# An input projection rewritten as seven half-size block products, with half of its outputs turned afterwards

## Chip, cores and metric

One core of a Trainium2 chip runs the kernel. The metric is the device time of one execution in microseconds (us), the median of several runs. TensorE (PE) does matrix products, and its weight loads are listed apart as PEld; VectorE is DVE, ScalarE is ACT, GpSimd is POOL, and SyncE (SP) issues most of the DMAs.

## Reference

The layer works on 2048 tokens of 1024 features, in float32:

```
mod = silu(c) @ w_ada + b_ada;  shift, scale, gate = split(mod, 3)
h = rms_norm(x, norm_g) * (1 + scale) + shift
u = h @ w_in                                   # 2048 x 1024 times 1024 x 8192
a_q, a_f, a_i, a_g, b_q, b_k, b_v, b_g = split(u)
o_a = rms_norm(hgrn2(silu(a_q), a_f, a_i)) * silu(a_g)
o_b = rms_norm(stick_breaking_attention(b_q, b_k, b_v)) * silu(b_g)
out = rms_norm(x + gate * (concat(o_a, o_b) @ w_out), final_g)
```

The change concerns `h @ w_in`, its outputs' activation and storing, and the making of `h`.

## The kernel before

The kernel runs five stages one after the other: `condition` (makes h), `project` (u), `hgrn`, `stick`, `output`. They hand data on through DRAM.

**Precision.** A float32 product is made of three reduced-precision ones. A number is rounded to a high part (ACT or POOL) and the rest is its difference to that (DVE or POOL); a product is hi\*hi + hi\*lo + lo\*hi.

**condition.** SP loads w_ada (12 pieces of 1 MB) and x (4 groups of 512 tokens). PE makes the modulation (L155). For each group ACT sums squares (L193), DVE scales x (L247), PE transposes it (L169), ACT makes the high part h_hi (L202), DVE makes the full h again (hx, L283) and POOL subtracts to h_lo (L295). h_hi and h_lo for all 2048 tokens stay in SBUF.

**project.** It goes through 32 chunks of 256 columns of w_in, in the order of the list PROJ: four kinds for which the output is feature by token (gq, gf, sq, sk), then four for which it is token by feature (gi, gg, sv, sg), four chunks each. A chunk has eight PSUM tiles of 128x512. For the first 16 chunks w is the stationary operand and 512 tokens move (L361, 24 matmuls a tile). For the last 16, h is stationary and 256 columns of w move (L370, 48 matmuls a tile). SP loads a chunk of 1 MB into the single buffer w_raw (L452), at the tile after POOL has finished splitting the chunk before; POOL splits it (L340, L342) into w_hi and w_lo, which have two buffers each. ACT applies the sigmoid or copies (L399 to L406), DVE finishes the output (L423 to L441), SP stores it (L477). DVE and ACT each take the tile that PE has just finished.

Eight PSUM banks hold eight tiles, so PE waits only for the bank of the tile eight before:

```
def tile(c, j, par, feature):
    pe.wait_ge(u_taken, 8 * c + j + 1)
...
if j == 1 and not (last and par == 1):
    sp.wait_ge(w_split, i * 4 + (2 * par + 2))
    load_w(i * 2 + (par + 1))
sp.wait_ge(u_taken, n + 9)
```

Some rows below are of the stage `output`, for operations of the same kinds: L1217 transposes, L1221 products of 128x512, L1277 rounding on ACT, L1358 the rest on DVE. L726 is a DVE multiplication in `hgrn`.

Of the kernel before, what the change touches and what calls it, by code (L numbers as in the profile page):

```python
# [26 lines left out]
P = 128  # L27
# [14 lines left out]
KO = 2 * D // P  # L42
NLEV = 8
# [19 lines left out]
def condition(nc, io, keep, h_hi, h_lo, w_raw, w_first, sv_rows):  # L63

    with ExitStack() as stack:
# [5 lines left out]
        slots = [n % 3 if n < n_mod + 1 else n % 2 for n in range(n_ada)]  # L71

        def slot(n):
            return ada[:, slots[n]] if slots[n] < 2 else w_raw[:, :, :]
# [5 lines left out]
        ada = m.sb("ada", [P, 2, KD, AC])  # L80
        xg = m.sb("xg", [P, 2, 4, D])
# [10 lines left out]
        hx = m.sb("hx", [P, 2, 512])  # L92
# [5 lines left out]
        x_in = [m.sem(f"x_in{i}") for i in range(2)]  # L98
# [13 lines left out]
        hx_ready = m.sem("hx_ready")  # L112
        lo_ready = m.sem("lo_ready")
        dve_step = m.sem("dve_step")

        with nc.Block() as block:
            @block.sync
            def _(sp):
# [5 lines left out]
                def load_x(g):  # L124
                    if g >= 2:
                        sp.wait_ge(xt_ready, KD * (g - 1))
                    src = io["x"][g * 512:(g + 1) * 512, :].rearrange("(b p) n -> p b n", p=P)
                    sp.dma_start(xg[:, g % 2], src).then_inc(x_in[g % 2], 16)
# [9 lines left out]
                for n in range(6, n_mod + 2):  # L138
                    load_ada(n)
                load_x(2)  # L140
                load_ada(n_mod + 2)
                load_ada(n_mod + 3)
                load_x(3)

                sp.wait_ge(mod_ready, [n for n in range(n_ada) if slots[n] == 2][-1] + 1)
                sp.dma_start(w_raw[:, :, :], io["w_in"][0]).then_inc(w_first, 16)

            @block.tensor
            def _(pe):
# [12 lines left out]
                for g in range(TG):  # L162
                    pe.wait_ge(xn_ready, 4 * (g + 1))
                    for k in range(KD):
                        n = g * KD + k
                        if n >= 4:
                            pe.wait_ge(hx_ready, n - 3)
                        for b in range(4):
                            mm = nc.tensor.transpose(xt_ps[n % 4][:, b * P:(b + 1) * P],  # L169
                                                     xg[:, g % 2, b, k * P:(k + 1) * P], keep["ident"][:, :])  # L170
                        mm.then_inc(xt_ready, 1)
                    modulation(n_mod + g)

            @block.scalar
            def _(act):
# [6 lines left out]
                act.dma_start(keep["g_hgrn"][:, :], io["g_hgrn"].partition_broadcast(P)).then_inc(wide_in, 16)  # L182
                act.dma_start(keep["g_stick"][:, :], io["g_stick"].partition_broadcast(P)).then_inc(wide_in, 16)
                act.dma_start(sv_rows[0:1, :], io["zero"]).then_inc(wide_in, 16)

                def squares(g):
                    act.wait_ge(x_in[g % 2], 16 * (g // 2 + 1))
                    if g >= 1:
                        act.wait_ge(var_ready, g)
                    for b in range(4):  # L190
                        if g or b:
                            act.wait_ge(sq_ready, 4 * g + b)
                        nc.scalar.activation(junk[:, :], xg[:, g % 2, b, :], ACT.Square,  # L193
# [4 lines left out]
                def high(g):  # L198
                    for k in range(KD):
                        n = g * KD + k  # L200
                        act.wait_ge(xt_ready, n + 1)
                        nc.scalar.activation(h_hi[:, k, g * 512:(g + 1) * 512], xt_ps[n % 4][:, :], ACT.Identity,  # L202
# [11 lines left out]
            def _(dve):  # L214
# [20 lines left out]
                def norm(g):  # L235
# [10 lines left out]
                    for b in range(4):  # L246
                        nc.vector.tensor_scalar(xg[:, g % 2, b, :], xg[:, g % 2, b, :], stat[:, 3, b:b + 1], None,  # L247
                                                ALU.mult).then_inc(xn_ready, 1)
# [27 lines left out]
                dve.wait_ge(wide_in, 64)  # L276
                for g in range(TG):
                    for k in range(KD):
                        n = g * KD + k
                        dve.wait_ge(hi_ready, n + 1)  # L280
                        if n >= 2:
                            dve.wait_ge(lo_ready, n - 1)
                        nc.vector.tensor_scalar(hx[:, n % 2, :], xt_ps[n % 4][:, :], mul[:, k:k + 1], shift[:, k:k + 1],  # L283
                                                ALU.mult, ALU.add).then_inc(hx_ready, 1)
                    take_mod(n_mod + g)
                    if 1 <= g < TG - 1:
                        norm(g + 1)

            @block.gpsimd
            def _(pool):  # L290
                for n in range(TG * KD):
                    g, k = n // KD, n % KD
                    pool.wait_ge(hx_ready, n + 1)
                    hi = h_hi[:, k, g * 512:(g + 1) * 512].bitcast(F32)
                    nc.gpsimd.tensor_tensor(h_lo[:, k, g * 512:(g + 1) * 512], hx[:, n % 2, :], hi,  # L295
                                            ALU.subtract).then_inc(lo_ready, 1)


# [5 lines left out]
def project(nc, io, keep, h_hi, h_lo, w_raw, w_first, scr):  # L304

    with ExitStack() as stack:
        m = Mem(nc, stack)
        w_hi = m.sb("w_hi", [P, 2, KD, WC], F32R)
        w_lo = m.sb("w_lo", [P, 2, KD, WC], F32R)
        st = m.sb("st", [P, 2, 512])  # L310
        st2 = m.sb("st2", [P, 2, 512])
        st_hi = m.sb("st_hi", [P, 2, 512], F32R)
        st_lo = m.sb("st_lo", [P, 2, 512], F32R)
        sg = m.sb("sg", [P, 2, 512])
        sg2 = m.sb("sg2", [P, 2, 512])
        u_ps = [m.ps(f"u_ps{i}", [P, 512]) for i in range(8)]

        w_in_sem = m.sem("w_loaded")
        w_high = m.sem("w_high")
        w_split = m.sem("w_split")  # L320
        u_ready = m.sem("u_ready")
        u_act = m.sem("u_act")
        u_taken = m.sem("u_taken")
        g_step = m.sem("g_step")
        staged = m.sem("staged")
        stored = [m.sem(f"stored{i}") for i in range(2)]
        passed = m.sem("w_passed")
        n_pair = NCH // 2

        def tiles():  # L330
            return [(par, j) for par in range(2) for j in range(8)]

        with nc.Block() as block:
            @block.gpsimd
            def _(pool):
                def chunk(c, par):
                    pool.wait_ge(w_in_sem, 16 * c)
                    pool.wait_ge(u_ready, 8 * c + 8)
                    nc.gpsimd.sem_inc(passed, 1)
                    nc.gpsimd.tensor_copy(w_hi[:, par], w_raw[:, :, :]).then_inc(w_split, 1)  # L340
                    pool.wait_ge(w_split, 2 * c + 1)
                    nc.gpsimd.tensor_tensor(w_lo[:, par], w_raw[:, :, :], w_hi[:, par].bitcast(F32),  # L342
                                            ALU.subtract).then_inc(w_split, 1)

                chunk(1, 1)
                with nc.gpsimd.Fori(1, n_pair) as i:
                    for par in range(2):
                        chunk(i * 2 + par, par)

            @block.tensor  # L350
            def _(pe):
                nc.tensor.sem_inc(u_ready, 16)

                def tile(c, j, par, feature):
                    pe.wait_ge(u_taken, 8 * c + j + 1)
                    if feature:
                        cg, tp = j // 4, j % 4
                        n = 0
                        for wt, ht in ((w_hi, h_hi), (w_hi, h_lo), (w_lo, h_hi)):
                            for k in range(KD):  # L360
                                mm = nc.tensor.matmul(u_ps[j][:, :], wt[:, par, k, cg * P:(cg + 1) * P],  # L361
                                                      ht[:, k, tp * 512:(tp + 1) * 512], start=(n == 0), stop=(n == 3 * KD - 1))
                                n += 1
                    else:
                        for b in range(2):
                            tb = 2 * j + b
                            n = 0
                            for wt, ht in ((w_hi, h_hi), (w_hi, h_lo), (w_lo, h_hi)):
                                for k in range(KD):
                                    mm = nc.tensor.matmul(u_ps[j][:, b * WC:(b + 1) * WC], ht[:, k, tb * P:(tb + 1) * P],  # L370
                                                          wt[:, par, k, :], start=(n == 0), stop=(n == 3 * KD - 1))
                                    n += 1
                    mm.then_inc(u_ready, 1)

                for half, feature in ((0, True), (1, False)):
                    with nc.tensor.Fori(half * n_pair // 2, (half + 1) * n_pair // 2) as i:
                        for par in range(2):
                            c = i * 2 + par
                            pe.wait_ge(w_split, 2 * c + 2)
                            for j in range(8):  # L380
                                tile(c, j, par, feature)

            @block.scalar
            def _(act):

                act.wait_ge(w_first, 16)
                for k in range(KD):
                    nc.scalar.activation(w_hi[:, 0, k, :], w_raw[:, k, :], ACT.Copy).then_inc(w_high, 1)
                for t, (name, feature, _) in enumerate(PROJ):
                    with nc.scalar.Fori(t * CH_T // 2, (t + 1) * CH_T // 2) as i:  # L390
                        for par, j in tiles():
# [1072 lines left out]
```

## Time and profile before

| | us |
|---|---|
| median of 3 runs | 3245.58 (3242.29 to 3245.82) |
| the profiled execution | 3247.25 |
| its span | 3245.5 |
| PE busy | 3064.1 (94%) |
| PEld busy | 2722.1 (84%) |
| DVE busy | 1500.2 (46%) |
| ACT busy | 970.9 (30%) |
| POOL busy | 492.1 (15%) |
| mean granted TensorE clock | 0.977 |

The span runs from the first to the last instruction of one execution; busy time is the time in which an engine had an instruction running, so parts of matmuls that overlap are counted once. A granted clock of 1.00 is the 2.4 GHz level, and a value between 0.5 and 1 is a mixture of that and 1.2 GHz over the stretch.

### The profile page before, as it was taken

The page shows a single profiled execution, that of the slowest core. Times are in us where ns is not written, and L with a number is a line of the kernel's source. Part 1 is how long each engine was busy: PE and PEld are TensorE (multiplying, and loading weights), DVE is VectorE, ACT ScalarE, POOL GpSimd, SP SyncE. Part 2 cuts the span into 40 slices and gives each one's busy share as a digit, 9 for nine tenths or more (in the row PEclk, how much of TensorE's full clock was granted, in tenths as well). Part 3 has the DMA queues.
Part 4 walks back from the last instruction along what each step waited for, and adds up shares of the span by engine and source line. Part 5 has one row for each costly group of instructions (what it writes and reads, how often), then busy time and mean ns, then how long its engine had stood idle before and what let it go on. Part 6 is the DMA issues. An engine that isn't in the chain of part 4 may idle for free. (4 is left out here: it accounts for less than half of the span.)

```text
span 3245.5 us, 56894 instructions
## 1 busy us (share of the span) xinstructions
PE 3064.1 (94%) x22432; PEld 2722.1 (84%) x22432; DVE 1500.2 (46%) x1651; ACT 970.9 (30%) x1749; POOL 492.1 (15%) x218
## 2 busy tenths in 40 slices
PE   7899999999999999999788886999999999889998
PEld 5688888888999999999688875887878888778887
DVE  4211221111112221122787885888778887663433
ACT  4211211111111111111011114777767777631111
POOL 3211111111111011100554451000000000000000
PEclk9999999999999999999899997999999999989999
DMA  7113444443222122221544309244533351052221
GB/s 281 50 67 97 122 123 122 120 120 111 73 73 69 60 72 71 68 67 52 190 157 149 113 21 215 65 102 98 131 89 80 95 131 40 24 188 107 84 97 39
DMA packets 217944, 327.14 MB, mean 101 GB/s; under 512 B 11680, under 2 KB 159520, under 8 KB 204960
## 3 DMA queue, kind: packets, MB, share of 16 engines
q1 hardware_dynamic: 217296, 324.08, 33.5%
q8 instruction: 114, 1.87, 0.2%
q10 hardware_dynamic: 464, 0.63, 0.1%
q14 instruction: 70, 0.57, 0.1%
HBM read 207.22 MB, written 117.44 MB: 100 GB/s over the span
## 5 line engine op out<-in xcount | busy, mean ns | idle before, releaser
L1096 DVE TENSOR_TENSOR_SCAN run<-akeep 128x768 f32<-128x768 f32 (+7 forms) x256 | 426.5, 1708 | 134.4 <-ACT akeep L1066 133.7
L1055 ACT ACTIVATE wt<-t_ps 128x512 f32<-128x512 f32 (+3 forms) x640 | 313.6, 534 | 144.6 <-PE t_ps L985 144.4
L985 PE MATMUL t_ps<-ident,run 128*128 128x128 f32 x2176 | 311.5, 278 | 7.0 <-DVE run L1096 6.3
L1066 ACT ACTIVATE akeep<-z_ps 128x1024 f32<-128x1024 f32 (+7 forms) x384 | 289.9, 779 | 75.6 <-PE z_ps L974 68.8
L370 PE MATMUL u_ps<-w_hi,h_lo 128*128 128x256 f32 x2048 | 287.5, 283 | 0.0
L370 PE MATMUL u_ps<-w_lo,h_hi 128*128 128x256 f32 x2048 | 287.5, 283 | 0.0
L370 PE MATMUL u_ps<-w_hi,h_hi 128*128 128x256 f32 x2048 | 287.5, 283 | 0.0
L1005 PE MATMUL o_ps<-wt,ad 128*64 128x128 f32 x4352 | 280.0, 277 | 5.5 <-issue 5.5
L985 PEld LDWEIGHTS t_ps<-ident,run 128*128 128x128 f32 x2176 | 245.1, 141 | 46.7 <-issue 28.3
L969 PE MATMUL z_ps<-ak,aq 128*128 128x512 f32 (+3 forms) x640 | 251.1, 392 | 33.9 <-DMA aq<-s_qlo 33.9
L643 PE MATMUL hps<-hq,hk 128*128 128x128 f32 x1792 | 219.5, 286 | 51.2 <-DVE hq L726 13.5
L1005 PEld LDWEIGHTS o_ps<-wt,ad 128*64 128x64 f32 x4352 | 233.8, 137 | 37.7 <-issue 37.7
L370 PEld LDWEIGHTS u_ps<-w_hi,h_hi 128*128 128x128 f32 x2048 | 264.3, 192 | 0.1
L370 PEld LDWEIGHTS u_ps<-w_hi,h_lo 128*128 128x128 f32 x2048 | 264.2, 192 | 0.0
L370 PEld LDWEIGHTS u_ps<-w_lo,h_hi 128*128 128x128 f32 x2048 | 264.2, 192 | 0.0
L643 PEld LDWEIGHTS hps<-hq,hk 128*128 128x128 f32 x1792 | 214.7, 201 | 55.8 <-issue 53.4
L361 PE MATMUL u_ps<-h_hi,w_hi 128*128 128x512 f32 x1024 | 254.7, 391 | 6.0 <-DVE w_lo L413 6.0
L361 PE MATMUL u_ps<-h_lo,w_hi 128*128 128x512 f32 x1024 | 254.0, 390 | 0.0
L361 PE MATMUL u_ps<-h_hi,w_lo 128*128 128x512 f32 x1024 | 252.9, 389 | 0.0
L974 PE MATMUL z_ps<-ak,aq 128*128 128x512 f32 (+3 forms) x640 | 252.2, 399 | 0.0
L1096 DVE TENSOR_TENSOR_SCAN run<-akeep,run 128x1024 f32<-128x1024 f32 (+1 forms) x128 | 228.4, 1825 | 45.8 <-ACT akeep L1066 45.8
L340 POOL CAST w_hi<-w_raw 128x2048 fp32r<-128x2048 f32 x31 | 58.8, 1895 | 1164.6 <-DMA w_raw<-in_w_in 1164.6
(140 smaller groups left out, 3824.5 us busy)
## 6 DMA issues: line engine op xcount, KB each, us to landing
w_raw<-in_w_in SPq DMA_DIRECT2D x32, 1024.0 KB, 5.5
aq<-s_qhi SPq DMA_DIRECT2D x64, 256.0 KB, 6.3
aq<-s_qlo SPq DMA_DIRECT2D x64, 256.0 KB, 6.8
o<-s_o SPq DMA_DIRECT2D x16, 1024.0 KB, 6.9
ada<-in_w_ada SPq DMA_DIRECT2D x9, 1024.0 KB, 8.5
xg<-in_x SPq DMA_DIRECT2D x4, 2048.0 KB, 11.0
s_gq<-st SPq DMA_DIRECT2D x32, 256.0 KB
s_gf<-st SPq DMA_DIRECT2D x32, 256.0 KB
```

The lines of the kernel that those rows point to most:

```text
L340: nc.gpsimd.tensor_copy(w_hi[:, par], w_raw[:, :, :]).then_inc(w_split, 1)
L361: mm = nc.tensor.matmul(u_ps[j][:, :], wt[:, par, k, cg * P:(cg + 1) * P], ht[:, k, tp * 512:(tp + 1) * 512], start=(n == 0), stop=(n == 3 ...
L370: mm = nc.tensor.matmul(u_ps[j][:, b * WC:(b + 1) * WC], ht[:, k, tb * P:(tb + 1) * P], wt[:, par, k, :], start=(n == 0), stop=(n == 3 * K ...
L643: mm = nc.tensor.matmul(out, k[:, e, toks], q[:, 2 * u + e, toks], start=True, stop=True)
L969: nc.tensor.matmul(zz, q_hi, kk, start=True, stop=False)
L974: mm = nc.tensor.matmul(zz, q_lo, kk, start=False, stop=True)
L985: mm = nc.tensor.transpose(t_ps[a % 2][:, j * P:(j + 1) * P], src[:, key + j * P:key + (j + 1) * P], keep["ident"][:, :])
L1005: mm = nc.tensor.matmul(o_ps[e * SD:(e + 1) * SD, cols], delta[:, b, key // P + j, e * SD:(e + 1) * SD], wt[:, a % 8, j * P:(j + 1) * P], ...
L1055: nc.scalar.activation(wt[:, a % 8, 0:wd], t_ps[a % 2][:, 0:wd], ACT.Identity, scale=-1.0, bias=1.0).then_inc(wt_ready, 1)
L1066: nc.scalar.activation(keepf[:, e, n % 2, 0:width], z_ps[e][:, 0:width], ACT.Sigmoid, scale=-SCALE).then_inc(keep_ready, 1)
L1096: nc.vector.tensor_tensor_scan(run[:, e, qb % 2, at0:at0 + width][:, ::-1], keepf[:, e, n % 2, 0:width][:, ::-1], keepf[:, e, n % 2, 0:width],
```

## The change

`w_in` is cut into blocks of 512 rows by 128 columns, four to a chunk (2 by 2), and h into blocks of 512 features by 512 tokens, four to a pass of 1024 tokens. A 2 by 2 block product is computed with seven products of blocks instead of eight, by sums and differences of the blocks on the way in and of the results on the way out. Each of the seven is again hi\*hi + hi\*lo + lo\*hi: 12 matmuls of 128x512, so a unit ("tile n" below) has 84 matmuls. There are 64 tiles: two passes over the 1024 tokens, 32 chunks each; w_in is loaded in each pass. All outputs are feature by token; for gi, gg, sv and sg PE transposes them in the middle of the next tile's products (`turn`), ACT copies the result out (`turned`), SP stores it.

- In `condition`, h is stored whole (no h_hi, h_lo). Token groups are taken in the order 2, 3, 0, 1; the first two go through four buffers hx to DRAM and are loaded again for the second pass. The x tiles have three buffers; L283 and L295 are gone.
- For each tile, SP loads four blocks of w (two DMAs of 512 KB), POOL makes four combinations (four operations of 128x512, each but one waiting for one before), ACT rounds the seven factors in three operations (`w_rounded`, 1024, 1536 and 1024 columns), DVE makes their rests (`w_rest`, the same three sizes).
- For each pass ACT rounds the seven h factors (2048 columns each), DVE makes three sums and six rests of that size, POOL one rest and one difference.
- For each tile DVE does five sums of 128x512 (PSUM and SBUF into SBUF) besides finishing the four outputs (`shape`).
- The loops are written out, without Fori.

```
+def combine_w(nc, pool, w_raw, t_done, n):
+    w = w_raw[:, n % 2]
+    nc.gpsimd.tensor_tensor(w[:, 3], w[:, 2], w[:, 0], ALU.subtract).then_inc(t_done, 1)
+    pool.wait_ge(t_done, 4 * n + 1)
+    nc.gpsimd.tensor_tensor(w[:, 1], w[:, 6], w[:, 3], ALU.subtract).then_inc(t_done, 1)
+    nc.gpsimd.tensor_tensor(w[:, 2], w[:, 6], w[:, 2], ALU.subtract).then_inc(t_done, 1)
+    pool.wait_ge(t_done, 4 * n + 3)
+    nc.gpsimd.tensor_tensor(w[:, 4], w[:, 5], w[:, 1], ALU.subtract).then_inc(t_done, 1)
...
+            def _(pool):                      # project
+                def build(p):
+                    pool.wait_ge(h_high, 7 * p + 1)
+                    nc.gpsimd.tensor_tensor(hc_lo[:, 0], x[:, 1], hc_hi[:, 0].bitcast(F32), ALU.subtract).then_inc(h_first, 1)
+                    pool.wait_ge(h_sum, 3 * p + 1)
+                    nc.gpsimd.tensor_tensor(x[:, 2], x[:, 1], x[:, 2], ALU.subtract).then_inc(h_third, 1)
+                build(0)
+                for n in range(1, NT):
+                    pool.wait_ge(w_in_sem[n % 2], 32 * ((n + 1) // 2))
+                    combine_w(nc, pool, w_raw, t_done, n)
+                    if n == NCH:
+                        build(1)
...
+            def _(pe):
+                def product(n, j):
+                    pe.wait_ge(w_split, 3 * n + PIECE_OF[j] + 1)
...
+                    if j == 4:
+                        pe.wait_ge(sum_ready, 5 * n + 2)
...
+                for n in range(NT):
+                    for j in range(NP7):
+                        product(n, j)
+                        if n >= 1 and not feature(n - 1) and 1 <= j <= 4:
+                            turn(n - 1, j - 1)
...
+            def _(act):
+                def w_rounded(n):
+                    act.wait_ge(t_done, 4 * (n + 1))
...
+                    for a, b in PIECES:
+                        nc.scalar.activation(w_hi[:, n % 2, a:b], w_raw[:, n % 2, a:b], ACT.Copy).then_inc(w_high, 1)
...
+                for n in range(NT):
+                    if n == NCH:
+                        for j in range(1, NP7):
+                            h_rounded(1, j)
+                    act.wait_ge(u_ready, 7 * n + 1)
+                    wait_free(act, n, 1)
+                    nc.scalar.activation(s_buf[1][:, n % 2, :], b1[n % 2][:, :], ACT.Copy).then_inc(one_ready, 1)
+                    if n >= 1 and not feature(n - 1):
+                        for q in range(4):
+                            turned(n - 1, q)
+                    if n + 1 < NT:
+                        w_rounded(n + 1)
+                    if n == NCH - 1:
+                        h_rounded(1, 0)
+                    for q in range(4):
+                        shape(n, q)
...
+            def _(dve):
+                h_sums(0)
+                for piece in range(3):
+                    w_rest(0, piece)
+                h_rests(0)
+                for n in range(NT):
+                    if n == NCH:
+                        h_sums(1)
+                        h_rests(1)
+                    summed(n, 0)
+                    summed(n, 1)
+                    summed(n, 2)
+                    summed(n, 3)
+                    shape(n, 0)
+                    if n + 1 < NT:
+                        w_rest(n + 1, 0)
+                        w_rest(n + 1, 1)
+                    shape(n, 1)
+                    shape(n, 2)
+                    if n + 1 < NT:
+                        w_rest(n + 1, 2)
+                    summed(n, 4)
+                    shape(n, 3)
...
+            def _(sp):
+                def load_w(n):
+                    if n >= 2:
+                        sp.wait_ge(u_ready, 7 * (n - 1))
...
+                for n in range(NT):
+                    if n + 1 < NT:
+                        load_w(n + 1)
+                    back = n - 1 if n >= 1 and not feature(n - 1) else None
+                    for i in range(4):
+                        if n == NCH - 1:
+                            load_h(i)
+                        if back is not None:
+                            store(back, i)
+                    if feature(n):
+                        for q in range(4):
+                            store(n, q)
```

`sum_ready` counts the sums of `summed`, `w_split` the operations of `w_rest`, `fa_ready` and `fd_ready` the outputs that ACT and DVE have done. `store(n, q)` waits until output q of tile n is finished; gf, sq and sk store two arrays for each output, gq one. For them the gate buffer sg has two places, each free again when its store has landed. A `summed(n, 2)` feeds output 0, `summed(n, 4)` output 3.

## Rows read from the trace of the kernel before

**Rows 1.** The page: busy time of TensorE, and its granted clock in 40 slices.

```profile
PE 3064.1 (94%) x22432; PEld 2722.1 (84%) x22432; DVE 1500.2 (46%) x1651; ACT 970.9 (30%) x1749; POOL 492.1 (15%) x218
...
PEclk9999999999999999999899997999999999989999
```

**Rows 2.** Busy time by stretch: length, PE, PEld, DVE, ACT, POOL, clock, DMA share, GB/s.

```profile
80.00:100.00 20.00, 11.52 (x56) 9.87 (x54) 12.66 (x22) 9.78 (x16) 13.04 (x12) 0.83 0.00 0
...
120.00:796.00 676.00, 676.00 (x2984) 559.95 (x2983) 110.67 (x156) 91.19 (x157) 104.09 (x32) 1.00 0.36 109
800.00:1530.00 730.00, 730.00 (x6071) 729.38 (x6070) 139.84 (x187) 75.79 (x127) 97.71 (x30) 1.00 0.20 68
```

**Rows 3.** Timeline of PE, seam and end of the projection: start, length, engine, line.

```profile
796.32 1.98 PE L361 MATMUL u_ps<-h_hi,w_lo 128*128 128x512 f32 x8
...
803.57 1.12 PE L370 MATMUL u_ps<-w_hi,h_hi 128*128 128x256 f32 x8
...
1539.88 1.12 PE L370 MATMUL u_ps<-w_lo,h_hi 128*128 128x256 f32 x8
```

**Rows 4.** The chain that ended last, in `output`: start, length, what.

```profile
3001.97 1.75 PE ot_ps L1217 x16
3003.72 21.78 PE y_ps L1221 x96
3025.50 1.75 PE ot_ps L1217 x16
```

**Rows 5.** Timeline from the third token group to the start of the projection.

```profile
72.32 5.57 ACT L202 ACTIVATE h_hi<-xt_ps,shift,mul 128x512 fp32r<-128x512 f32 x7 [4.99 <-PE xt_ps L169]
...
89.14 5.69 ACT L202 ACTIVATE h_hi<-xt_ps,shift,mul 128x512 fp32r<-128x512 f32 x7 [4.99 <-PE xt_ps L169]
...
90.84 9.87 POOL L295 TENSOR_TENSOR h_lo<-hx,h_hi 128x512 fp32r<-128x512 f32 x8 [6.96 <-DVE hx L283]
...
101.04 2.56 ACT L388 ACTIVATE w_hi<-w_raw 128x256 fp32r<-128x256 f32 x8 [5.24 <-PEq L116]
...
104.39 3.77 PE L361 MATMUL u_ps<-h_hi,w_hi 128*128 128x512 f32 x8 [5.95 <-DVE w_lo L413]
...
110.87 1.99 PE L361 MATMUL u_ps<-h_hi,w_lo 128*128 128x512 f32 x8
```

**Rows 6.** Single lines: duration in ns, shortest/median/longest, first and last start.

```profile
L342 POOL TENSOR_TENSOR w_lo<-w_raw,w_hi x31: 4598/4613/4629, 124.3 to 1465.0; 128x2048 fp32r<-128x2048 f32 x31
...
L429 DVE TENSOR_SCALAR st<-sg,lb x32: 485/487/4859, 288.4 to 456.7; 128x512 f32<-128x512 f32 x32
...
L726 DVE TENSOR_TENSOR hq<-hq,hf x8: 2264/2274/2284, 1568.6 to 1857.6; 128x2048 f32<-128x2048 f32 x8
...
L1277 ACT ACTIVATE wo_hi<-wo_raw x16: 1055/1062/1067, 2852.5 to 2880.0; 128x1024 fp32r<-128x1024 f32 x16
...
L1358 DVE TENSOR_TENSOR wo_lo<-wo_raw,wo_hi x16: 1218/1225/1227, 2853.6 to 2881.1; 128x1024 fp32r<-128x1024 f32 x16
```

**Rows 7.** Groups of instructions by line: busy us, mean ns, idle before and releaser.

```profile
L295 POOL TENSOR_TENSOR h_lo<-hx,h_hi 128x512 fp32r<-128x512 f32 x32 | 39.5, 1278 | 60.8 <-DVE hx L283 60.8
...
L439 DVE TENSOR_TENSOR st<-u_ps,sg 128x512 f32<-128x512 f32 x64 | 44.3, 691 | 266.1 <-ACT sg L406 266.1
...
L404 ACT ACTIVATE sg<-u_ps 128x512 f32<-128x512 f32 x64 | 38.3, 598 | 330.4 <-PE u_ps L370 330.4
```

**Rows 8.** DMA issues: line, count, KB each, median us from issue to landing.

```profile
w_raw<-in_w_in SPq DMA_DIRECT2D x32, 1024.0 KB, 5.5
...
ada<-in_w_ada SPq DMA_DIRECT2D x9, 1024.0 KB, 8.5
...
hk<-s_gk SPq DMA_DIRECT2D x8, 1024.0 KB, 4.8
...
out<-wo_raw SPq DMA_DIRECT2D x16, 512.0 KB, 2.7
```

**Rows 9.** Timeline of SP's queue in the projection.

```profile
203.57 0.36 SPq L452 DMA_DIRECT2D w_raw<-in_w_in  x1
```

More of the change, by code:

```diff
@@ L42 @@
 KO = 2 * D // P
+KH = KD // 2
+NP7 = 7
+HALF = SEQ // 2
 NLEV = 8
@@ L275, in _ @@
                 dve.wait_ge(col_ready, 1)
-                dve.wait_ge(wide_in, 64)
+                dve.wait_ge(wide_in, 80)
                 for g in range(TG):
[L278 to L285, printed above, removed]
@@ L319, in project @@
         w_high = m.sem("w_high")
         w_split = m.sem("w_split")
-        u_ready = m.sem("u_ready")
[L322 to L331, printed above, removed]
+        h_raw = [m.sem(f"h_raw{i}") for i in range(4)]
@@ new lines, in project @@
+        h_high = m.sem("h_high")
+        h_first = m.sem("h_first")
+        h_third = m.sem("h_third")
+        h_sum = m.sem("h_sum")
+        h_split = m.sem("h_split")
+        u_ready = m.sem("u_ready")
+        one_ready = m.sem("one_ready")
+        sum_ready = m.sem("sum_ready")
+        fa_ready = m.sem("fa_ready")
+        fd_ready = m.sem("fd_ready")
+        t_ready = m.sem("pt_ready")
+        t_taken = m.sem("pt_taken")
+        u_stored = [[m.sem(f"u_stored{q}{j}") for j in range(2)] for q in range(4)]
@@ new lines, in project, with kind, feature @@
+        sg_stored = [m.sem(f"sg_stored{j}") for j in range(2)]
+        stt_stored = [m.sem(f"stt_stored{j}") for j in range(2)]
+        NT = 2 * NCH
+        PIECES = [(0, 2), (2, 5), (5, 7)]
+        PIECE_OF = [0, 0, 1, 1, 1, 2, 2]
+        SUMS = {0: 3, 1: 4, 3: 5}
+        QUAD = {0: (1, 1), 1: (1, 0), 2: (0, 0), 3: (0, 1)}
+        def kind(n):
+            return PROJ[n % NCH // CH_T]
+        def feature(n):
+            return kind(n)[1]
+        fa_at, fd_at, t_at, u_st, sg_st, sg_last, sg_free = {}, {}, {}, {}, {}, {}, {}
@@ new lines, in project @@
+        fa_n = fd_n = t_n = 0
+        for n in range(NT):
+            name = kind(n)[0]
+            for q in range(4):
+                if name not in ("gi", "sv") or q == 2:
+                    fa_n += 1
+                    fa_at[n, q] = fa_n
+                if name not in ("gi", "sv"):
+                    fd_n += 1
+                    fd_at[n, q] = fd_n
+                    sg_free[n, q] = sg_last.get(q % 2)
+                    sg_last[q % 2] = (n, q)
+                if feature(n):
+                    u_st[n, q] = sum((x, q) in u_st for x in range(n % 2, n, 2)) + 1
+                    if name != "gq":
+                        sg_st[n, q] = sum(y[1] % 2 == q % 2 for y in sg_st) + 1
+                else:
+                    t_n += 1
+                    t_at[n, q] = t_n
@@ new lines, in _ @@
+                for n in range(NT):
+                    if n + 1 < NT:
[6 more added lines that the diff above has]
+                            store(back, i)
+                    if feature(n):
+                        for q in range(4):
+                            store(n, q)
@@ L489, in hgrn @@
+                for q in range(4):
+                    store(NT - 1, q)
+                for q in range(4):
+                    for e in range(2):
+                        sp.wait_ge(u_stored[q][e], 16 * max(v for (n, r), v in u_st.items() if r == q and n % 2 == e))
+                for e in range(2):
+                    sp.wait_ge(sg_stored[e], 16 * max(v for (n, q), v in sg_st.items() if q % 2 == e))
+                    sp.wait_ge(stt_stored[e], 16 * (len(t_at) // 2))
 def hgrn(nc, io, keep, scr, o_scr):
```

468 lines of the change are left out of this document (288 added, 180 removed).

## The prediction

> **What bounds the kernel now.** I read the page first: TensorE is busy 94% of the span at nearly the full granted clock, VectorE, the next engine, 46% [rows 1]. Then the busy time by stretch: from 120 to 796 us (outputs feature by token) and from 800 to 1530 us (token by feature) PE is busy all the time at clock 1.00, the 2.4 GHz level, while DVE and ACT are busy under a fifth of it [rows 2]. So the projection costs what its matmuls cost, and fewer matmuls pay in full as long as PE stays fed. Then PE's timeline for the pace: 32 matmuls of 512 columns from 796.32 to 803.57 us are 226.6 ns each; the 6144 of 256 columns from 803.57 to 1539.88 + 8 x 0.12 = 1540.84 us are 120.0 ns each [rows 3], with the weight loads busy throughout [rows 2]. Two of 256 columns cost 240 ns where one of 512 costs 226.6: the second half is the dearer one.
>
> **Matmuls.** At 226.6 ns the first half's 3072 matmuls are 696.1 us; counted back from 803.57 the projection effectively starts at 107.5 (really at 104.4; the first 16 matmuls, after 6 us of PE idle, take 6.5 us, 0.4 us each, the 1.2 GHz level [rows 5]). It thus takes 1540.8 - 107.5 = 1433.3 us. After: 64 tiles x 84 = 5376 matmuls x 226.6 ns = 1218.2 us. Transposes: 32 turned tiles x 16; the output stage runs 16 of them in 1.75 us between products of 21.78 us, and the two add up to the period of 23.53 [rows 4], so 56.0 us. A split into four groups of four might cost a little more; I add nothing. A plain tile is 19.05 us, a turned one 20.8. **Difference: 1274.2 - 1433.3 = -159.1 us**, if PE never waits.
>
> **condition.** A token group takes 16.8 us (72.32 to 89.14 [rows 5]); its chain is ACT's rounding, ACT's squares, DVE's scaling, the transposes, and it stays. Gone is POOL's tail: the last L295 ends at 100.7, some 5 us after ACT's last rounding, and the project block starts at 101. The first group, now paced by ACT and stores (2.7 us landing of a larger one [rows 8], four buffers: about 0.9 us each) instead of by POOL at 1.23, gains no more than the 1 to 2 us that the second loses to its own stores. The block starts near 95. The combination of w for tile 0 is covered by the groups.
>
> **The first tile.** Prices: DVE 2.27 us for 2048 columns, 1.22 for 1024 [rows 6], 1.7 for 1536 between them; POOL 4.61 for 2048 [rows 6], 1.28 for 512 [rows 7]; ACT 1.06 for 1024 [rows 6], about 1.95 for 2048, 0.60 for 512 [rows 7]. In order on DVE before the sums that product 4 needs: two sums (4.5), three rests of w (4.0), four rests of h (9.0), a difference and two rests (6.8), two sums of 512 (1.4, [rows 7]): 26 us, and at least 3 more for POOL's difference in the chain: 29. That is the lower bound. The upper one comes from POOL and DVE in each other's way: a DVE operation of 487 ns once took 4.859 us, as long as POOL's 4.61 [rows 6]. POOL has two operations of 4.6 us and four of 1.28 here, so up to 10 more. By the Trainium skill, "SBUF — State Buffer", "Who interferes with whom", a DVE instruction with two SBUF inputs or in a two-port mode and a POOL instruction reading SBUF exclude each other; that would give the upper bound, and the rule without it the lower. I take +7 (nearer the row of 4.859): product 4 at 95 + 36 = 131, tile 0 ends 8.2 later at 139.2, effective start 120.1 instead of 107.5: **+12.6 us** (6 to 16).
>
> **The seam of the passes.** After tile 31 the same DVE work stands ahead of product 4 of tile 32, less the rests of w but behind 2 us of tile 31's last output: product 4 near 26.5 us after the seam instead of 11 to 12, so +14, and with POOL up to +24. **+20 us.**
>
> **The loop that I think decides.** Follow the order on each queue in a feature tile n. SP issues load_w(n+1) only after store(n-1,3), which waits for DVE's last output of tile n-1; call that moment 0. SP: hop 0.15, a store, the load (an issue is 0.36 [rows 9], some 0.45 with the gap): 0.6. The 1 MB lands in 5.5 [rows 8], 0.2 more for the second DMA: 6.3. POOL: four operations of 1.28 [rows 7] = 5.1, to 11.4. ACT rounds (0.94 + 1.38 + 0.94, the pace behind durations of 1.06 for 1024) to 14.7, and only then does output 0 (0.60): 15.4. DVE: output 0 (0.69), rest of w, first piece (1.22): **17.3, when PE may begin tile n+1**. Second piece 1.7, outputs 1 and 2 1.4, third piece 1.15, last sum 0.7: 22.3. ACT 0.6, DVE 0.7: **23.6, the last output of tile n, which releases load_w(n+2)**. This is a ring of one tile that doesn't contain PE: it turns in 23.6 us where PE needs 19.05. For gq. For gf the last output has two stores ahead of the load (+0.4, and 256 KB more in the queue, +0.6), ACT two sigmoids on outputs 0 and 3 (+1.2), DVE two operations instead of one (0.49 + 0.54, +0.3 x 4), and output 2 waits for output 0's store (+0.4): 27.4. For sq and sk: second store +1.0, waits for the stores of sg +0.7: 25.3. PE then idles in each feature tile. The first and the last of a pass's 16 feature tiles nearly escape; 3 x 4.5 + 4 x 8.3 + 7 x 6.2 = 90, plus 1, and two passes give **+182 us**. The mean ring of the 28 tiles is 25.5 us.
>
> The unknowns: the load lands in 4.8 (hk, an idle queue) to 8.5 us (ada, a full one) [rows 8], 28 tiles x -0.7 to +2.8 = -20 to +78; I take 5.7, as the projection's own row has it. POOL's 512 is a quarter of L342 (1.15) to 1.28: -14 us. A store's landing is not shown for 256 KB; 0 to 2 us per gf, sq, sk tile: -15 to +30. POOL works at 6.3 to 11.4, when DVE only reads PSUM with one SBUF operand, so I charge no collisions.
>
> **Turned tiles.** Here load_w goes at the tile's start (its stores come a tile later) and is covered. ACT however must copy out all four turned outputs before it rounds w: the fourth is turned at 5 x 2.72 + 1.75 = 15.35; ACT 0.6 + 3.3 + 0.6, DVE 0.7 + 1.2: 21.8 against 20.8. For gg and sg, 16 tiles: **+17 us** (0 to 30). gi and sv have no output 0 in that place: nothing.
>
> **Clock.** After 6 us of PE idle the first 16 matmuls ran at 1.2 GHz, and lost 16 x 0.18 = 2.8 us [rows 5]. In the loop a slow start is covered: 19.05 + 2.8 = 21.9 is still under 23.6. A whole tile at that level would be 84 x 0.4 = 34 us and is not.
>
> The last four outputs and their longer tail: +1. hgrn, stick and output are as they were.
>
> **Sum:** -159.1 + 12.6 + 20 + 182 + 17 + 1 = +73.5 us. Span 3245.5 becomes 3319; the profiled execution's own time is 3247.25, 1.7 above the median shown, so against the median 3319.5.
>
> **Rivals.**
> 1. *The loads are hidden as meant.* Were the ring under 19 us (a landing near 1 us, or another order on SP), only ramps and gates would remain: -159.1 + 12.6 + 20 + 17 + 1 = -108.5, or 3137. For it: w has two buffers now, POOL is 15% busy [rows 1]. Against it: 4.8 us is the shortest landing of 1 MB in the rows [rows 8], and ACT and DVE alone hold 12 us of the ring. By the Trainium skill, "Trainium Kernel Development and Optimization", "Best Practices", double buffering overlaps DMA with compute; here the second buffer waits behind the stores on SP. Chance 0.07.
> 2. *The other side: the ring binds, but is shorter, and the kernel gains.* The sum is +73.5; 28 tiles must each be 2.6 us shorter to undo that, a mean ring under 22.9 us instead of 25.5. Its place is the link from the load to POOL's last combination (11.4 us of it). With the landing at 4.8 and POOL at 4.6, and no waits for the stores of sg, the ring is 1.9 us shorter on average, -53 us; both ramps at their lower bounds give 13 more and the gate tiles 17: 73.5 - 83 = -9.5, or 3236. Every one of them has to come out at its favourable end. Chance 0.10.
> 3. *The clock decides.* If with 4 to 8 us of idle per tile the lower level holds through the feature tiles, as in the stretch of clock 0.83 where PE was busy 58% [rows 2], PE needs 34 us: +8.5 x 28 = +240, or 3555. With a mixture at 0.83 it needs 23 and hides. Chance 0.03.
> 4. *The load lands late* (8.5, stores ahead of it in the queue): +78, about 3398. Chance 0.07.
>
> **Numbers.** Forecast (slower, the ring) 0.73, its own range 3265 to 3375. The range reaches down into rival 2 and a little into rival 4: 3235 to 3380 leaves out rivals 1 and 3, half of the others and the forecast's tails, some 0.2. What a measurement of this kernel can tell from no change is about 0.2%, 6.5 us. Faster: rival 1 and most of 2, 0.14; same 0.03; slower 0.83.
>
> **What would show it.** Tile starts on PE 23 to 27 us apart in feature tiles, about 22 or less in turned ones; PE waiting at product 0 for DVE's rest of w; ACT's w_rounded waiting for POOL; POOL waiting for the load; SP's load_w about 0.6 us behind the last output. Matmuls at 226 ns, 84 in 19 us. Wrong would be: feature tiles at 19 to 20 us (rival 1), the clock under 0.8 there (rival 3), landings over 7 us (rival 4), or a wait on sums at products 1 to 6 in mid-pass, which I have nowhere.

## Result and the profile after

The changed kernel takes 3365.45 us (3362.61 to 3368.54, 4 runs) against 3245.7 us: ratio 1.0371, 95% interval 1.0353 to 1.0389. It is slower by 120 us; the forecast was 74 slower, and 3365 lies inside its range. The profiled execution has a span of 3366.2 us.

The page of the changed kernel, for [rows 1]:

```profile
PE 2992.5 (89%) x19104; PEld 2509.7 (75%) x19104; DVE 1887.7 (56%) x2013; ACT 1279.8 (38%) x2090; POOL 615.1 (18%) x384
...
PEclk8798899999898898999899997999999999989999
```

PE has less to do, but is busy 89% instead of 94%, and in the slices of the projection the clock row has 8 and 9 where it had only 9. Busy time by stretch, changed kernel, columns as in [rows 2]: the first stretch holds feature tiles, the second turned ones, the third feature tiles of the second pass.

```profile
180.00:500.00 320.00, 266.79 (x1057) 214.69 (x1057) 126.91 (x167) 83.12 (x114) 64.35 (x51) 0.90 0.41 118
560.00:880.00 320.00, 313.11 (x1481) 255.50 (x1479) 129.41 (x144) 113.99 (x156) 78.79 (x60) 1.00 0.33 106
1000.00:1300.00 300.00, 244.76 (x976) 196.66 (x975) 120.64 (x157) 81.59 (x112) 56.30 (x44) 0.90 0.43 120
```

PE is idle for 17 to 18% of the feature stretches and for 2% of the turned one. DVE, the next engine, is busy 40% there and the DMA engines 41 to 43%, so none of them is full either. That points to a chain through several engines. Who ended PE's idle time between 80 and 1680 us (waits: line, waited for, us in total, times, longest):

```profile
PE b_ps L470 <- DVE w_lo L581: 164.9, 48, 15.1
...
PE b_ps L470 <- DVE u L650: 7.8, 2, 5.9
```

L581 is `w_rest`, L650 `summed`. The sums, on which five of the seven products wait, hold PE twice; the rest of the weights does it 48 times.

One turn of the ring itself, from the last gf tile (7) to the first sq tile (8) of the changed kernel (timeline; the waits for PE's own matmuls left out):

```profile
328.90 2.89 DVE L581 TENSOR_TENSOR w_lo<-w_raw,w_hi 128x1024 fp32r<-128x1024 f32 x2
...
330.17 2.08 PE L470 MATMUL b_ps<-hc_hi,w_hi 128*128 128x512 f32 x4 [6.02 <-DVE w_lo L581]
...
334.61 1.22 DVE L581 TENSOR_TENSOR w_lo<-w_raw,w_hi 128x1024 fp32r<-128x1024 f32 x1
...
338.05 0.54 DVE L630 TENSOR_SCALAR u<-u,lb 128x512 f32<-128x512 f32 x1
...
338.98 0.43 SPq L705 DMA_DIRECT2D s_gk<-sg  x1
...
339.45 0.46 SPq L681 DMA_DIRECT2D w_raw<-in_w_in  x1
...
346.53 1.29 POOL L315 TENSOR_TENSOR w_raw<-w_raw 128x512 f32<-128x512 f32 x1 [22.96 <-DMA w_raw<-in_w_in]
...
351.83 3.37 ACT L501 ACTIVATE w_hi<-w_raw 128x1024 fp32r<-128x1024 f32 x3 [13.73 <-POOL w_raw L320]
355.11 1.13 ACT L536 ACTIVATE sg<-u 128x512 fp32r<-128x512 f32 x2
355.75 0.69 DVE L625 TENSOR_TENSOR u<-u,sg 128x512 f32<-128x512 f32 x1 [8.81 <-ACT sg L536]
356.36 2.88 DVE L581 TENSOR_TENSOR w_lo<-w_raw,w_hi 128x1024 fp32r<-128x1024 f32 x2
...
357.63 2.08 PE L470 MATMUL b_ps<-hc_hi,w_hi 128*128 128x512 f32 x4 [5.98 <-DVE w_lo L581]
```

DVE finishes the last output of tile 7 at 338.6. SP issues the load 0.9 us later, behind two stores. POOL sits idle until the load has landed (7.1 us), ACT until POOL is done (5.3), and ACT rounds all of the weights (3.3) before it takes the next output; DVE does that output and the first piece of the rests, and PE begins at 357.63. From start to start of tile 8 it is 27.5 us, of which PE needs 19.05. The outputs at 355.11 and 355.75 are already those of sq, which cost DVE less than gf's.

Where the time went, by the starts of the tiles' first matmuls on PE's timeline:

| term | forecast | measured |
|---|---|---|
| matmuls and transposes | -159.1 | -159.1, the base that the rows below are counted over |
| preparation and tile 0: tile 1 begins at 156.3, less 19.05, against 107.5 | +12.6 | +29.7 |
| seam: tiles 31 and 32 take 27.8 + 49.2 instead of 2 x 20.8 | +20 | +35.4 |
| the ring: tiles 1 to 16 and 33 to 48 over 19.05 each | +182 | +191.4 |
| turned tiles 17 to 30 and 49 to 63 over 20.8 each | +17 | +23.5 |
| tail and the stages behind | +1 | +0.7 |
| sum | +73.5 | +121.6 (spans: +120.7; the tiles' rounded lengths make the difference) |

Mean tile by kind, from start to start, without tiles 0, 31 and 32 (and without the first turned tile of a pass): gq 22.8, gf 27.0, sq and sk 25.3, gi and sv 21.1, gg and sg 22.2 us.

### The profile page after: what moved, and what is told of

It reads as the page before. It is cut to its first block and busy times, and to the rows that moved or that the text cites. A ratio compares the mean times of both kernels' runs of the same rounds, so it can differ in the third digit from the quotient of the medians.

```text
span 3366.2 us, 50012 instructions
## 1 busy us (share of the span) xinstructions
PE 2992.5 (89%) x19104; PEld 2509.7 (75%) x19104; DVE 1887.7 (56%) x2013; ACT 1279.8 (38%) x2090; POOL 615.1 (18%) x384
## 5 line engine op out<-in xcount | busy, mean ns | idle before, releaser
L470 PE MATMUL b_ps<-hc_hi,w_hi 128*128 128x512 f32 x1792 | 526.9, 418 | 188.9 <-DVE w_lo L581 164.9
L470 PEld LDWEIGHTS b_ps<-hc_hi,w_hi 128*128 128x128 f32 x1792 | 339.6, 198 | 273.9 <-DVE w_lo L581 185.1
L650 DVE TENSOR_TENSOR u<-b_ps,u 128x512 f32<-128x512 f32 x320 | 220.5, 689 | 516.7 <-PE b_ps L470 516.3
L470 PE MATMUL b_ps<-hc_lo,w_hi 128*128 128x512 f32 x1792 | 506.5, 406 | 0.0
L470 PE MATMUL b_ps<-hc_hi,w_lo 128*128 128x512 f32 x1792 | 495.1, 399 | 0.0
L470 PEld LDWEIGHTS b_ps<-hc_lo,w_hi 128*128 128x128 f32 x1792 | 354.4, 198 | 80.0
L470 PEld LDWEIGHTS b_ps<-hc_hi,w_lo 128*128 128x128 f32 x1792 | 349.2, 195 | 78.5
L501 ACT ACTIVATE w_hi<-w_raw 128x1024 fp32r<-128x1024 f32 (+1 forms) x192 | 216.0, 1190 | 409.8 <-POOL w_raw L320 409.8
L315 POOL TENSOR_TENSOR w_raw<-w_raw 128x512 f32<-128x512 f32 x64 | 84.4, 1319 | 1169.2 <-DMA w_raw<-in_w_in 1169.2
L581 DVE TENSOR_TENSOR w_lo<-w_raw,w_hi 128x1024 fp32r<-128x1024 f32 (+1 forms) x192 | 269.2, 1430 | 28.3 <-ACT w_hi L501 27.2
L1250 PEld LDWEIGHTS o_ps<-wt,ad 128*64 128x64 f32 x4352 | 233.8, 137 | 36.5 <-issue 36.5
```

The lines of the kernel that those rows point to most:

```text
L470: mm = nc.tensor.matmul(bank[:, :], wt[:, n % 2, j, k * P:(k + 1) * P], ht[:, j, k * 512:(k + 1) * 512], start=(j < 4 and c == 0), stop=(c ...
L581: nc.vector.tensor_tensor(w_lo[:, n % 2, a:b], w_raw[:, n % 2, a:b], w_hi[:, n % 2, a:b].bitcast(F32), ALU.subtract).then_inc(w_split, 1)
L650: nc.vector.tensor_tensor(dst, bank[:, :], add, ALU.add).then_inc(sum_ready, 1)
L1250: mm = nc.tensor.matmul(o_ps[e * SD:(e + 1) * SD, cols], delta[:, b, key // P + j, e * SD:(e + 1) * SD], wt[:, a % 8, j * P:(j + 1) * P], ...
```

## Experiments

Theory A is the ring: load, POOL, ACT, DVE's outputs, store, and again load on SP, without PE. Its rival is that PE, its clock or DVE's load sets these 23 to 27 us, and the load comes late only because all is late. Theory B is about the starts: collisions of POOL with DVE, and a DMA order in the preparation. The times of e1 and e8_all are medians of four executions. Those of the others are one execution each, and four of the changed kernel lie 6 us apart, so there the tiles' lengths in the trace carry more than the total.

**Cutting the ring (e1_load_on_act).** The two load DMAs move from SP to ACT's queue. Tile 1's load stands at the head of ACT's program.

```
 # SP
-                    if n + 1 < NT:
-                        load_w(n + 1)
 # ACT, at its outputs of tile n
                     for q in range(4):
+                        if q == 3 and n + 2 < NT:
+                            load_w(n + 2)
                         shape(n, q)
```

> Edit: the two load DMAs of a tile's weights are issued from ACT's queue, just ahead of ACT's output 3 of the tile before, instead of from SP behind that tile's stores. They still wait for the tile's last product (the raw weights lie where PE reads w_lo). Nothing else is changed. Theory (a ring of one tile: load, POOL, ACT, DVE's last output, store, load): the ring is cut, since the load now follows PE's tile end directly; from there to the first piece of w_rest it is 0.6 + 5.7 + 5.1 + 3.3 + 0.6 + 0.7 + 1.2 = 17.2 us, under PE's 19.05, so plain tiles come 19.1 us apart and the 191 us that feature tiles lose in the changed kernel are gone: about 3176 us, PE no longer idle at product 0. Rival (PE, its clock or DVE's load sets the 23 to 28 us, and the load only happens to be late): tiles stay over 22 us and the time over 3300 us.

3214.67 us, ratio to the kernel before 0.9904 (0.9888 to 0.9921): with nothing but two DMAs issued from another place the change becomes a gain of 1.0%, 151 us under the changed kernel, of which tiles 1 to 16 and 33 to 48 make 149.8. gq tiles come 19.07 us apart, PE's own 19.05. The rival falls. But gf stayed at 21.6 and sq and sk at 20.1, and the result is 39 us over what I wrote. PE's waits of this kernel from 80 to 1600 us name another line (L660 is `summed` there, L591 `w_rest`):

```profile
PE b_ps L470 <- DVE u L660: 36.3, 21, 7.0
PE b_ps L470 <- DVE w_lo L591: 32.8, 19, 10.9
```

and the timeline of a gf tile names the cause:

```profile
260.16 0.63 ACT L547 ACTIVATE sg<-u 128x512 f32<-128x512 f32 x1 [5.18 <-DMA s_gk<-sg]
...
261.35 0.49 DVE L639 TENSOR_SCALAR sg<-sg,lb 128x512 f32<-128x512 f32 x1 [3.66 <-ACT u L548]
...
261.61 1.37 POOL L315 TENSOR_TENSOR w_raw<-w_raw 128x512 f32<-128x512 f32 x1 [16.85 <-DMA w_raw<-in_w_in]
261.75 1.51 DVE L640 TENSOR_SCALAR u<-u,lb 128x512 f32<-128x512 f32 x1
...
263.19 2.26 DVE L660 TENSOR_TENSOR u<-b_ps,u 128x512 f32<-128x512 f32 x3
...
264.80 1.16 PE L470 MATMUL b_ps<-hc_hi,w_hi 128*128 128x512 f32 x4 [1.71 <-DVE u L660]
```

ACT waits 5.2 us for a store out of the two-place buffer sg to land; behind the output that it holds up, DVE does three sums at once, and PE's fifth product (264.80) has waited 1.7 us for the second of them. Some of this is a collision that the delay brings about: the held-up output now falls on POOL's first combination, and L640 takes 1.51 us, where in other turns it takes 0.54.

**Four places for sg (e7_act_load_sg4).** On top of e1: `sg = m.sb("sg", [P, 4, 512])`, an own place and semaphore for each output.

> Edit, on top of e1: only the four places for the gate buffer sg. Theory: sg's stores, not PE or the load, make the gf tiles 21.6 and the sq and sk tiles 20.1 us; with four places both fall to 19.1 to 19.5: 33 us, about 3182 us. Rival (the load, slower beside the stores, still sets these tiles): under 10 us gained.

3178.32 us, 36 under e1 where 33 were expected; gf tiles 19.15, sq and sk 19.17. PE's waits from 95 to 1600 us keep the rests of w (32.9 us, most of it at the starts and in gg and sg tiles), while those for sums fall to 8.7:

```profile
PE b_ps L470 <- DVE u L660: 8.7, 2, 6.8
```

So the two rings together, the load's and sg's, account for the feature tiles to 0.1 us a tile.

**Shortening the ring by less (e1b_load_before_last_store).** SP issues the load ahead of store 3 instead of behind it.

> Edit: on SP the load of the next weights goes ahead of the store of output 3 instead of behind it; it stays behind the stores of outputs 0 to 2. Theory (the ring): the ring now closes over output 2, so it is shorter by what DVE and ACT do between outputs 2 and 3: third piece 1.2, sum 0.7, ACT 0.6, output 0.7, together 3.2 us (gf 4.3 with its two more, sq and sk 3.5). From the tiles measured in the changed kernel (gq 22.9, gf 27.6, sq and sk 25.2 us) that makes gq 19.7, gf 23.3, sq and sk 21.7: 28 tiles save some 110 us, about 3255 us. Rival (PE or DVE-bound): no change, 3365 us.

3284.59 us: 81 us gained, where 110 were expected. gq 20.3, gf 23.7, sq and sk 23.2, so the direction and most of the size hold for gq and gf, and sq and sk are 1.5 us over. In these the load now goes right behind four stores of 256 KB, and POOL starts 7.7 us after its issue on average, against 6.6 in the changed kernel, which is 1.1 of the 1.5:

```profile
424.59 0.33 SPq L704 DMA_DIRECT2D s_khi<-sg  x1
424.96 0.43 SPq L705 DMA_DIRECT2D s_klo<-u  x1
...
425.44 0.46 SPq L704 DMA_DIRECT2D s_khi<-sg  x1
425.94 0.46 SPq L705 DMA_DIRECT2D s_klo<-u  x1
...
426.44 0.45 SPq L681 DMA_DIRECT2D w_raw<-in_w_in  x1
...
435.24 1.29 POOL L315 TENSOR_TENSOR w_raw<-w_raw 128x512 f32<-128x512 f32 x1 [18.74 <-DMA w_raw<-in_w_in]
```

**Lengthening the ring (e2_pool_op_twice).** POOL's first combination is made a second time, with its wait, on the changed kernel.

```
     nc.gpsimd.tensor_tensor(w[:, 3], w[:, 2], w[:, 0], ALU.subtract).then_inc(t_done, 1)
+    pool.wait_ge(t_done, 5 * n + 1)
+    nc.gpsimd.tensor_tensor(w[:, 3], w[:, 2], w[:, 0], ALU.subtract).then_inc(t_done, 1)
```

> Edit: POOL does its first combination of a tile's weights (128x512) twice, with a wait between; POOL is busy 18% of the span. Theory (the ring holds POOL's four operations in series): each feature tile is longer by one operation and its hop, 1.33 us, turned tiles are not: 28 tiles x 1.33 = 37 us, plus some 2 to 4 in the first tiles of the passes, about 3406 us. Rival (POOL's work is covered): under 5 us more.

3413.61 us, 48 more than the changed kernel. gq, gf and sq/sk tiles are longer by 1.5, 1.5 and 1.3 us, gi/sv and gg/sg by 0.0. An engine that is busy 18% of the span passes every added operation on in full, and only where the ring runs. Of the 48 us, the 42 that tiles 1 to 15 and 33 to 47 show are the firm part.

**Less work for PE (e3_two_thirds_matmuls).** The products leave out w_lo x h_hi, 56 matmuls a tile instead of 84.

> Edit: the products leave out w_lo x h_hi, so a tile has 56 matmuls instead of 84 (12.7 us of PE instead of 19.05); all other work stays. Theory (the ring doesn't contain PE): feature tiles of the middle of a pass stay at 23, 27.6 and 25.2 us within 0.5; only turned tiles shrink, from 21.0 to about 14.8 (gi, sv) and from 22.2 to about 17.5 (gg, sg): some 165 us, with 10 in the first tiles, so about 3190 us, with a lower granted clock. Rival (PE bounds the feature tiles too): they lose 6.3 us each as well, about 3010 us.

3225.91 us. Feature tiles: 22.9, 27.0 and 25.0 us, within 0.3 of the changed kernel's with a third of the matmuls gone; turned tiles 15.4 (gi, sv) and 18.8 (gg, sg). So PE doesn't bound the feature tiles. The sum is 36 us over what I wrote: the turned tiles shrank by 0.6 to 1.3 less than expected, and the starts of the passes by little. The clock of a stretch of feature tiles of this kernel:

```profile
260.00:500.00 240.00, 139.58 (x504) 109.67 (x504) 91.85 (x120) 64.92 (x88) 50.28 (x40) 0.76 0.42 118
```

PE spends about half of it at 1.2 GHz, and the tiles are no longer for it.

**The preparation (e4_stores_first).** SP's order on the changed kernel:

```
                 store_h(0)
+                store_h(1)
                 load_x(3)
                 load_ada(n_mod + 2)
                 load_ada(n_mod + 3)
-                store_h(1)
```

> Edit, on the changed kernel itself: in the preparation, SP issues the second token group's eight stores of h ahead of the load of the fourth group and of the last two pieces of w_ada. Theory: these stores waited behind 4 MB of loads in the queue, and ACT, with four buffers hx, sat 11.5 us for one; that goes, and the projection begins some 11 us earlier: about 3354 us. Rival (the fourth group, now loaded later, takes the time back): less than 4 us.

3354.97 us, 10.5 less; the first product begins at 111.5 instead of 121.8, which is 10.3 of it. ACT's waits of the changed kernel from 40 to 110 us had shown it:

```profile
ACT hx L226 <- DMA s_h<-hx: 16.4, 4, 11.5
```

**The starts of the passes (e5_h_on_dve).** POOL's two operations of 128x2048 go to DVE, on the changed kernel:

```
-                    nc.gpsimd.tensor_tensor(hc_lo[:, 0], x[:, 1], hc_hi[:, 0].bitcast(F32), ALU.subtract).then_inc(h_first, 1)
-                    nc.gpsimd.tensor_tensor(x[:, 2], x[:, 1], x[:, 2], ALU.subtract).then_inc(h_third, 1)
+                    nc.vector.tensor_tensor(hc_lo[:, 0], x[:, 1], hc_hi[:, 0].bitcast(F32), ALU.subtract).then_inc(h_first, 1)
+                    nc.vector.tensor_tensor(x[:, 2], x[:, 1], x[:, 2], ALU.subtract).then_inc(h_third, 1)
```

> Edit, on the changed kernel itself: the two POOL operations of 128x2048 at each start of a pass (4.6 us each) are done by DVE (2.3 us each) instead. Theory (a DVE operation with two SBUF inputs and a POOL operation exclude each other in time): DVE gets 4.6 us more work at each start but loses the waits, one of its sums took 6.49 us instead of 2.28: product 4 of tile 0 begins 35.5 us after the block's start instead of 38.5, the seam likewise shorter, 4 to 8 us in all, about 3359 us, and L601 takes 2.3 us. Rival (they don't exclude each other; the 6.49 us has another cause): each start is 4.6 us longer on DVE's chain, about 3374 us.

3359.1 us, 6.3 less than the changed kernel, which is about what its four executions lie apart; the trace is firmer. The seam's two tiles take 71.7 instead of 77.0 us, tile 0 begins 1.9 us sooner and is 1.8 shorter. DVE has more to do at the starts and is done sooner. The start of the projection, first in the changed kernel, then in this one (timelines):

```profile
107.45 2.29 DVE L597 TENSOR_TENSOR h_raw<-h_raw 128x2048 f32<-128x2048 f32 x1 [0.33 <-PEq L125]
...
109.42 4.70 POOL L428 TENSOR_TENSOR hc_lo<-h_raw,hc_hi 128x2048 fp32r<-128x2048 f32 x1 [58.92 <-ACT hc_hi L518]
109.78 6.49 DVE L601 TENSOR_TENSOR h_raw<-h_raw 128x2048 f32<-128x2048 f32 x1
114.08 6.55 POOL L430 TENSOR_TENSOR h_raw<-h_raw 128x2048 f32<-128x2048 f32 x1
```

```profile
107.63 2.29 DVE L593 TENSOR_TENSOR h_raw<-h_raw 128x2048 f32<-128x2048 f32 x1 [0.32 <-PEq L125]
109.84 2.29 DVE L585 TENSOR_TENSOR hc_lo<-h_raw,hc_hi 128x2048 fp32r<-128x2048 f32 x1
112.04 2.28 DVE L599 TENSOR_TENSOR h_raw<-h_raw 128x2048 f32<-128x2048 f32 x1
```

L601 (L599 in the other kernel) took 6.49 us beside POOL's 4.70 and takes 2.28 without it: 4.70 + 2.28 is 6.98, and the two had begun 0.4 us apart. By the Trainium skill, "SBUF — State Buffer", "Who interferes with whom", a DVE instruction with two SBUF inputs and a POOL instruction that reads SBUF exclude each other; the trace agrees, 6.49 against 2.28 us.

**Together (e8_all).** e1, four places for sg, e4, e5, and ACT rounds the next weights ahead of the last turned output:

```
-                        for q in range(4):
+                        for q in range(3):
                             turned(n - 1, q)
                     if n + 1 < NT:
                         w_rounded(n + 1)
+                    if n >= 1 and not feature(n - 1):
+                        turned(n - 1, 3)
```

> Edit, on top of e1: four places for the gate buffer sg instead of two; ACT rounds the next weights before it copies out the last of the four turned outputs instead of behind it; the two big POOL operations on h go to DVE; in the preparation the stores of the second token group go ahead of the load of the fourth and of two pieces of w_ada. Theory: e1 left 21.6 (gf) and 20.1 us (sq, sk) a tile because DVE's sums stand behind an output whose sg place waits for its store to land; with four places these become 19.1 to 19.5: 8 x 2.3 + 16 x 0.9 = 33 us. gg and sg tiles go from 22.2 to 21.0: 16 x 1.2 = 19 us. The preparation: 11 us. The two starts of a pass: 3 to 6 us each, 9. From e1's 3215 some 72 less: about 3143 us. Rival (the collisions move rather than go, DVE then being the bound at the starts): no better than 3165 us.

3139.95 us, ratio to the kernel before 0.9677 (0.9661 to 0.9693). Plain tiles are at 19.05 (gq), 19.23 (gf) and 19.10 us (sq, sk) in the mean, and turned ones inside a pass at 21.02 or 21.03. Its PE line and clock:

```profile
PE 2922.7 (93%) x19104; PEld 2471.1 (79%) x19104; DVE 1883.4 (60%) x2017; ACT 1274.9 (41%) x2090; POOL 591.3 (19%) x380
...
PEclk9799999999999999998999979999999999899999
```

## Why the prediction held, and where it missed

**Matmul count and pace: right.** A product of 12 matmuls takes 2.72 us where it doesn't wait and the granted clock is at the 2.4 GHz level. Four transposes between products cost 0.49 us in the middle ones (3.21 - 2.72) instead of the 0.44 I charged, and a turned tile without a wait takes 21.02 instead of 20.8: the "little more" for splitting into groups is 0.2 us a tile, about 7 of the 23.5 us of that term.

**The ring: right, its sum in part by luck.** Forecast 23.6, 27.4 and 25.3, measured 22.8, 27.0 and 25.3 us; +182 against +191. But the 14 tiles of a pass that I had counted in full (1 to 14, 33 to 46) lost 173.6 us against 180, and the ones behind them (15, 16, 47 and 48), for which I had 2 us in all because the last should "nearly escape", lost 17.7: tiles 15 and 47 took 24.8 and 24.7 us, a full turn. The 9 us are an error of -6 and one of +16. e1, e2 and e3 show that the ring is the cause, from three sides. Its single terms erred both ways: the load took 5.8 to 6.6 us from issue to POOL's start where I had 5.7, POOL 5.3 where I had 5.1; for gq, the way from the last output to the load took 0.4 where I had 0.6, and the way from PE's start to the last output 5.9 where I had 6.3. Rival 1 needed a ring under 19 us and had nothing of it; rival 2 needed every term at its best, and the two terms of its link came out at or over my value.

**gg and sg: right**, 22.2 against 21.8; in e8_all they are at 21.0.

**Clock: right in effect.** After waits of 2.9 to 7.3 us in the feature tiles the first product took 4.2 to 5.3 us instead of 2.72, once 2.9. In tile 8 it ran from 330.17 to 335.14, beginning at a granted clock of 0.50, the 1.2 GHz level:

```profile
330.00:333.00 3.00, 2.83 (x7) 2.25 (x8) 2.64 (x4) 0.37 (x1) 0.00 (x0) 0.50 0.52 156
```

Behind the ring this cost nothing: the tile still ended before the next piece of the rests was there.

**The step that failed: "The first group ... gains no more than the 1 to 2 us that the second loses to its own stores", and with it "the block starts near 95".** It started at 107.4. I had counted the stores of the second group at their landing time and not at their place in SP's queue: SP issues the fourth group's x (2 MB) and two pieces of w_ada (2 MB) just ahead of them, and ACT waited 11.5 us for one of four buffers. I had walked SP's order for w, a load behind stores, and not for h, stores behind loads. The changed kernel, in the preparation:

```profile
54.15 0.45 SPq L138 DMA_DIRECT2D xg<-in_x  x1
54.64 1.03 SPq L131 DMA_DIRECT2D ada<-in_w_ada  x2
...
55.71 15.94 SPq L144 DMA_DIRECT2D s_h<-hx  x8
...
68.53 2.79 ACT L226 ACTIVATE hx<-xt_ps,shift,mul 128x512 f32<-128x512 f32 x4 [11.53 <-DMA s_h<-hx]
```

e4 starts the first product 10.3 us sooner with the order alone.

**Mis-sized: the collisions at the starts.** I took +7 of "up to 10" for tile 0, and 6 over the lower bound at the seam. Product 4 began 38.5 us after the block's start (145.93 - 107.45) instead of 36, so tile 0 was 2.5 over; its last three products took 10.4 us instead of 8.2, beginning at 1.2 GHz after the wait. With the 12.4 us of the late block these are the 17 us by which that term was short. At the seam I also had them fall only on the sums of h. But POOL's first operation of the second pass runs while DVE still finishes tile 31:

```profile
877.74 1.90 ACT L518 ACTIVATE hc_hi<-h_raw 128x2048 fp32r<-128x2048 f32 x1
...
879.72 4.50 POOL L428 TENSOR_TENSOR hc_lo<-h_raw,hc_hi 128x2048 fp32r<-128x2048 f32 x1 [11.95 <-ACT hc_hi L518]
...
880.19 4.58 DVE L633 SCALAR_TENSOR_TENSOR u<-u,g_stick,sg 128x512 f32<-128x512 f32 x1 [5.96 <-ACT sg L543]
884.69 2.88 DVE L581 TENSOR_TENSOR w_lo<-w_raw,w_hi 128x1024 fp32r<-128x1024 f32 x2
```

An operation of 0.75 us took 4.58, and the rest of the weights for tile 32 stood behind it: tile 32 began 27.8 us after tile 31 instead of 22.2. Of these 5.6 us, 3.8 are the collision. The other 1.8 are ACT's: its rounding of the next pass's first h factor (L518, 1.90 us) stands ahead of its outputs of tile 31, and so the output that DVE waits for came later. That is 5.6 us of the 15 by which the seam was under-sized. (Another 1.4 us is tile 31's own wait as a gate tile.) In tile 32 product 1 began 18.5 us after product 0 and product 4 36.5 us after it, where the +20 stood for 32.5; the three products from there took 12.6 us where 8.6 are their own. These two 4.0 are the rest of the 15. e5, which moves POOL's two operations, gives 5.3 us of the seam back. The traces also price POOL's four combinations of the next tile: DVE's four rests of h took 13.13 us beside them, and 8.90 in e5, where they had run earlier.

```profile
901.10 13.13 DVE L590 TENSOR_TENSOR hc_lo<-h_raw,hc_hi 128x2048 fp32r<-128x2048 f32 x4 [4.49 <-POOL h_raw L430]
```

**Two sums in the prediction are off**, and neither moves a bound. With 5.7 us as the load's own term, landings of 4.8 to 8.5 us give -25 to +78 us, not -20 to +78; rival 3 comes to 3558 us, not 3555.

**Missed in the working of e1:** the wait for sg's store, which I had charged with 0.4 to 0.7 us a tile inside the ring, bounds the tiles by itself once the load is out of the way (21.6 and 20.1 us). A wait that is cheap beside a longer one isn't a small wait.

**Chances.** The forecast had 0.73 and a range of its own of 3265 to 3375; the measured time lies at its upper end, 46 us over the point forecast. Most of that, some 38 us, comes from terms outside the ring: the preparation, the seam and the turned tiles.

## What to carry to other kernels

Count what a change takes off the bounding engine, and then walk each queue in its program order for one turn of the new loop: where a load is issued behind a store that waits for the last output, and that output stands behind work on the loaded data, a second buffer hides nothing, and the ring's length, not any engine's busy share, is the tile's time.

The Trainium skill, "Trainium Kernel Development and Optimization", "Best Practices", advises double buffering to overlap DMA with compute; here it did so in the feature tiles only from the moment the load had a queue position that didn't depend on the tile's own output (e1, 151 us). Test such a ring by lengthening a link on an idle engine and by taking work off the supposedly bounding one; here two such runs (e2 and e3) told it from a kernel that TensorE bounds.

## What the runs showed of the hardware beyond what was expected

- Whether DVE is held up beside POOL depended on the operands. A product with both inputs in SBUF took 1.76 us instead of 0.75 beside a POOL operation (863.49 us, L633), and the POOL operation that began during it (L318) took 1.75 instead of 1.28. A sum with one operand in PSUM, beside that same L318, kept its 0.68 (865.17 us, L650). A DVE operation with a single SBUF array and constants, L640 in e1, was held up too: 1.51 us instead of 0.54.

```profile
863.42 1.28 POOL L317 TENSOR_TENSOR w_raw<-w_raw 128x512 f32<-128x512 f32 x1
863.49 1.76 DVE L633 SCALAR_TENSOR_TENSOR u<-u,g_stick,sg 128x512 f32<-128x512 f32 x1 [0.70 <-ACT sg L543]
...
864.66 1.75 POOL L318 TENSOR_TENSOR w_raw<-w_raw 128x512 f32<-128x512 f32 x1
...
865.17 0.68 DVE L650 TENSOR_TENSOR u<-b_ps,u 128x512 f32<-128x512 f32 x1
```

- The same 1 MB load is usable 5.0 to 5.2 us after its issue in turned tiles and 7.7 us behind four stores on the same queue (e1b). In e1, issued from ACT's queue while SP's stores were under way, it took 7.1 to 7.2 in gf, sq and sk tiles, against 6.4 to 6.6 in the changed kernel: another queue changed when the load may begin, and made it no shorter.
